# The inverse stage's DFT in one partition half instead of two, and a filter load issued later

## The reference

```python
z = short_conv(u @ w_in + b_in, conv_w, conv_b)
x0, x1, v = jnp.split(z, 3, axis=-1)
s = v * x1
g = hyena_filter(L, ...)                       # (2L, D), L = 1024
y = irfft(rfft(s, n=2L, axis=1) * rfft(g, n=2L, axis=0), n=2L, axis=1)[:, :L]
y = (y + s * skip) * x0
return y @ w_out + b_out
```

## Time and profile before

| | us |
|---|---|
| median of 3 runs | 2532.4 |
| lowest, highest | 2531.71, 2537.66 |
| the profiled execution, its own time | 2537.66 |
| its span in the trace | 2535.2 |
| TensorE busy | 2429.3 (96%) |
| VectorE, GpSimd, ScalarE busy | 1124.9, 705.3, 634.2 |
| `sfwd` ends, `spec` runs | about 336, then to 526.7 |
| `inv` runs (TensorE) | 537.6 to 564.9 |

### The profile page before, as it was taken

How to read it: one execution, slowest core, us unless ns; L and a number is a source line. 1 busy time by engine, 2 the same in 40 slices (tenths; PEclk the granted TensorE clock), 3 DMA queues, 4 the chain that set the end, 5 groups by cost and what they waited for, 6 DMA issues and landing times.

```text
span 2535.2 us, 28807 instructions
## 1 busy us (share of the span) xinstructions
PE 2429.3 (96%) x11294; PEld 1959.1 (77%) x11294; DVE 1124.9 (44%) x1181; ACT 634.2 (25%) x768; POOL 705.3 (28%) x394
## 2 busy tenths in 40 slices
PE   7999999979999999999998899999999999999996
PEld 5767766547888888888887698989897887778885
DVE  6755543254266116622347763627272123420533
ACT  4433423342211000100113544444453001111111
POOL 2221233322233333333334122121212332333331
PEclk9999999999999999999999899999999999999998
DMA  4122354681222122211112202011113322111331
GB/s 148 34 100 100 117 190 158 196 236 42 75 92 90 50 75 99 83 50 66 47 47 73 92 26 74 26 67 33 67 33 119 138 79 67 54 42 66 99 117 66
DMA packets 69969, 217.62 MB, mean 86 GB/s; under 512 B 6662, under 2 KB 16584, under 8 KB 69642
## 3 DMA queue, kind: packets, MB, share of 16 engines
q1 hardware_dynamic: 57002, 178.88, 21.4%
q10 hardware_dynamic: 12896, 37.75, 4.0%
HBM read 171.52 MB, written 45.09 MB: 85 GB/s over the span
## 4 chain that ended last, share of the span: by engine, by line
PE 72%; DVE 4%; ACT 1%; issue 0%; ACTq 0%; DVEq 0%
PE ps L1208 61%; PE ps L541 5%; DVE T L1888 1%; PE ps L1479 1%; PE ps L588 1%; PE ps L609 1%; PE ps L608 1%; PE ps L570 1%; PE ps L607 1%; PE ps L1230 0%; DVE X L2227 0%; DVE XN L1918 0%; PE ps L1239 0%; PE ps L512 0%; ACT T L1771 0%; DVE H L1911 0%
## 5 line engine op out<-in xcount | busy, mean ns | idle before, releaser
L1208 PE MATMUL ps<-H,whi 128*128 128x512 f32 x4000 | 1086.6, 394 | 21.9 <-DVE H L1955 13.1
L1208 PEld LDWEIGHTS ps<-H,whi 128*128 128x128 f32 x4000 | 751.2, 189 | 195.1 <-issue 25.1
L1162 POOL CAST whi<-wraw 128x1024 fp32r<-128x1024 f32 x190 | 201.3, 1059 | 1703.6 <-PE ps L1208 805.9
L1208 PE MATMUL ps<-H,wlo 128*128 128x512 f32 x2000 | 617.9, 390 | 0.0
L1164 POOL TENSOR_TENSOR wlo<-wraw,whi 128x1024 fp32r<-128x1024 f32 x194 | 492.1, 2536 | 58.4 <-ACT whi L675 43.1
L1208 PEld LDWEIGHTS ps<-H,wlo 128*128 128x128 f32 x2000 | 376.6, 188 | 78.9
L1208 PE MATMUL ps<-A,whi 128*128 128x512 f32 x1472 | 397.7, 393 | 8.9 <-DVE A L2259 4.9
L1208 PEld LDWEIGHTS ps<-A,whi 128*128 128x128 f32 x1472 | 278.1, 189 | 68.4 <-issue 5.3
L1208 PE MATMUL ps<-A,wlo 128*128 128x512 f32 x736 | 228.3, 392 | 0.0
L1208 PEld LDWEIGHTS ps<-A,wlo 128*128 128x128 f32 x736 | 139.2, 189 | 29.1
L2143 DVE TENSOR_TENSOR T<-ps,T 128x1024 f32<-128x1024 f32 x22 | 26.9, 1224 | 155.8 <-PE ps L1208 155.8
(11 more groups left out here) (337 smaller groups left out, 2500.8 us busy)
## 6 DMA issues: line engine op xcount, KB each, us to landing
wraw<-in_panels SPq DMA_DIRECT2D x181, 512.0 KB, 3.5
mw<-in_modp SPq DMA_DIRECT2D x24, 512.0 KB, 3.5
g<-gsp SPq DMA_DIRECT2D x16, 512.0 KB, 3.2
wraw<-g SPq DMA_DIRECT2D x16, 512.0 KB, 5.9
bs<-s SPq DMA_DIRECT2D x16, 512.0 KB, 4.9
y<-yi ACTq DMA_DIRECT2D x32, 256.0 KB, 5.2
kf<-in_kfft SPq DMA_DIRECT2D x16, 320.0 KB, 3.1
X<-in_xT SPq DMA_DIRECT2D x4, 1024.0 KB, 11.0
```

Of the source, the lines that this page charges most:

```text
L1162: nc.gpsimd.tensor_copy(whi[:, s, :, :], wraw[:, s, :, :]).then_inc(hi_made, 1)
L1208: last = mm(p[:, c * step:(c + 1) * step], w[:, ws, k, :], operand(act, a, k, c * step, step), start=(q == 0 and w is whi and a == 0), sto ...
```

## The change

The `rows` jobs write PSUM partitions 0 to 63 only: a job now covers 4 slices m of 256 channels instead of 8, so there are 16 jobs instead of 8, with 4 matmuls each instead of 8. The copy back writes partitions 0 to 63 of `YB`, one slice for one slice. A `tile` job becomes 16 transposes of 64 x 128 pieces instead of 8 of 128 x 128, with a 64 x 64 identity. The order becomes: rows x4 | rows rows tile rows rows tile, three times | tile tile. VectorE's work is unchanged.

In SP's queue `filter_rows(1)` moves from between `matrices(1)` and the stores of slices 14 and 15 to after `matrices(3)`, just ahead of `x0_weights(1)`.

```diff
--- before.py
+++ after.py
@@ -68,11 +68,12 @@
 
 
 
-INV = [("rows", 0, 256, 8 * _m) for _m in range(2)]
+INV = [("rows", 0, 256, 4 * _m) for _m in range(4)]
 for _c in range(1, 4):
-    for _m in range(2):
-        INV.append(("rows", 256 * _c, 256, 8 * _m))
-        INV.append(("tile", 2 * _c - 2 + _m))
+    for _m in range(4):
+        INV.append(("rows", 256 * _c, 256, 4 * _m))
+        if _m % 2:
+            INV.append(("tile", 2 * _c - 2 + _m // 2))
 INV += [("tile", 6), ("tile", 7)]
 
 
@@ -1011,7 +1012,6 @@
                     sp.wait_ge(aux_done, A0["sfwd"] + sfwd_aux("turn", PAIRS - 1))
                     for g in range(2):
                         matrices(g)
-                    filter_rows(1)
             for m in range(N2 - 4, N2):
                 sp.wait_ge(*sa_out(m))
 
@@ -1032,8 +1032,7 @@
                 signal_in(g)
                 matrices(g + 2)
                 if g:
-                    if g > 1:
-                        filter_rows(g)
+                    filter_rows(g)
                     if g in X0_AFTER:
                         skipped = g + 1
                         x0_weights(g)
@@ -1418,14 +1417,13 @@
                         k = c0 // 256
                         pe.wait_ge(x_in[k], 64)
                     for u in range(T // w):
-                        for h in range(2):
-                            last = mm(p[HALF * h:HALF * h + HALF, u * w:(u + 1) * w], cc("idft"),
-                                      YB[:, m0 + 2 * u + h, c0:c0 + w], start=True, stop=True)
+                        last = mm(p[0:HALF, u * w:(u + 1) * w], cc("idft"), YB[:, m0 + u, c0:c0 + w], start=True, stop=True)
                 else:
                     e, q = j[0], inv_rows(j[0])
                     pe.wait_ge(evac[slot("inv", q)], turn("inv", q) + 1)
-                    for m in range(PAIRS):
-                        last = nc.tensor.transpose(p[:, m * P:(m + 1) * P], YB[:, m, e * P:(e + 1) * P], ident)
+                    for m in range(N2):
+                        last = nc.tensor.transpose(p[:, m * HALF:(m + 1) * HALF], YB[0:HALF, m, e * P:(e + 1) * P],
+                                                   ident[0:HALF, 0:HALF])
                 last.then_inc(aux_done, 1)
             panel_jobs("wout", 2, A, ready=(y_lo, 0))
             project("first", 0, (n2.lo, 0))
@@ -1698,7 +1696,7 @@
 
                     c0, w, m0 = j
                     act.wait_ge(aux_done, A0["inv"] + o + 1)
-                    A_(YB[:, m0 // 2:m0 // 2 + T // w, c0:c0 + w], ps[slot("inv", o)][:, :].rearrange("p (a b) -> p a b", b=w),
+                    A_(YB[0:HALF, m0:m0 + T // w, c0:c0 + w], ps[slot("inv", o)][0:HALF, :].rearrange("p (a b) -> p a b", b=w),
                        ACT.Copy).then_inc(evac[slot("inv", o)], 1)
 
                     if o and INV[o - 1][0] == "tile":
```

## The result

The changed kernel is slower: 2550.24 us median of 4 runs (2546.87 to 2550.8) against 2533.43 of 4 (2531.71 to 2537.66), a ratio of 1.0061, 95% interval 1.0049 to 1.0075, which is 12 to 19 us. Timed again later with the experiments it came to 1.0058 (1.0044 to 1.0071). The forecast was 2553.9 in a range of 2544 to 2560.

What follows compares the result with a forecast made beforehand. TensorE, busy 96% of the span, was taken as the bound. Inverse stage 12.7, late load 7.2 and half clock 1.6 summed to 21.5 us, giving a 2553.9 us median; own range 2549 to 2557, stated range 2544 to 2560.

Steps and rivals of the forecast that it cites:

- What bounds the stage: Inverse stage: TensorE's cycle grows from 2.90 to 5.45 us, above VectorE's 3.77 a tile, so TensorE becomes the bound.
- The lost pairing: Inverse-stage rows jobs: without the other half beside them, records cost 0.213 us each instead of 0.105 (upper bound 0.25).
- The transposes: Inverse-stage tiles: 16 narrow transposes at 0.107 us each, 1.71 us a tile against 0.86; lower bound 0.053 each.
- The case of cheap transposes: Rival, inverse stage: narrow transposes cost half, so the stage's 12.7 us becomes 7.4; total 2548.6 us; chance 0.13.
- ScalarE stays hidden: Inverse stage: 8 extra evacuations of 1.02 us give ScalarE 4.2 us of a 5.45 us cycle, so they stay hidden.
- The seam: End of the inverse stage, where the first panel's part k = 6 waits: moves 12.7 us later (+1/-1.5).
- The load: Second filter-spectra group: moved filter_rows(1) lands at 346.3, split at 349.8, so TensorE starts 7.2 us later (5.5 to 8.4).
- The clock after the stall: Second filter-spectra group: TensorE restarts at half clock for 3.3 us, costing 1.6 us (bounds 0 and 1.7).
- The load was not hidden: Rival at the second filter-spectra group: load arrives before 342.6, TensorE isn't held; sum 12.7, 2545.1 us; chance 0.06.
- The pairing was real: Rival, inverse-stage rows jobs: pairing did nothing, one half runs at 0.107; sum 11.8, 2544.2 us; chance 0.06.
- The clock did not stay low: Rival, inverse stage: clock stays low with half the array unused, 39 us more; 2593 us; chance 0.07.
- absorbed: Rival, after the convolution: later TensorE waits, 14.1 us at L1230, swallow the delay; not slower, 2532.4 us; chance 0.03.

Runs made afterwards that it cites:

- s10: Changed kernel plus 11 matmuls on constants in TensorE's idle time ahead of the inverse stage; ratio 1.0047 (1.0033 to 1.0061) against the kernel before.
- s3: Kernel before, with each rows job's four matmuls of partition half 0 first, then half 1's four, instead of alternating; ratio 1.0008 (0.9999 to 1.0017).
- s4: Kernel before, paired rows jobs kept, but each half copied separately into partitions 0 to 63 and 16 narrow transposes a tile; ratio 0.9990 (0.9978 to 1.0001).
- s11: Changed kernel with the load left early and copies into both partition halves, so 8 wide transposes a tile; ratio 1.0031 (1.0018 to 1.0045) against the kernel before.
- s5: Changed kernel with the load left early and plain matmuls by the 64 x 64 identity replacing transposes; ratio 1.0132 (1.0113 to 1.0150) against the kernel before.
- s1: Kernel before with only filter_rows(1) moved later in SP's queue, inverse stage untouched; ratio 1.0025 (1.0013 to 1.0037).
- s8: Kernel before plus 11 matmuls on constants in TensorE's idle 10.9 us ahead of the inverse stage; ratio 1.0021 (1.0012 to 1.0029).

## Why the prediction was right

The forecast of the time was right, and so were its two main mechanisms. One term, the transposes, was wrong in its reasoning, and the signs below show it.

**What bounds the stage.** Right. VectorE's 3.77 us a tile was the bound before, TensorE's cycle after. The first six `rows` jobs took 12.03 us to the first transposes, forecast 12.0 (its term for the half clock at the start, 1.4, is the 1.5 that s10 takes away).

**The lost pairing** (0.213 a record, bounds 0.105 and 0.25). Right: 3.67 us for 16 records is 0.219 apart, s3 shows the cause with one edit to the order alone, and s4 and s11 divide the rest of the new form from it.

**The transposes.** This is the term that was mis-sized. I took 0.107 a record from L1328, with a lower bound of 0.053; it is 0.067. L1328 is a plain matmul, and s5 shows that the form makes the difference: the same operands cost 0.113 as a plain matmul. The failed step is "with one column to stream, the weight load sets this rate, and the new transposes load 128 columns each": what limits the plain matmul didn't limit the transpose, and the 0.107 of the wide transposes that seemed to agree was no proof of the same limit. Per tile it makes 1.06 us instead of 1.71, a cycle of 4.74 instead of 5.45, and the sixth tile 37.45 - 28.84 = 8.6 us later in the stage instead of 12.6. The case of cheap transposes, which put this at 7.4, was rated 0.13; the truth lies between the two and nearer to it.

**ScalarE stays hidden.** Right for the cycle and wrong at its end. The forecast counted its load (4.2 us, of a cycle that came out at 4.74) and not its order: the copy of the last `rows` job stands behind a rounding copy and a skip term, and the seventh tile waits 1.22 us for it.

**The seam.** Forecast 12.7 us, measured 8.0 between the two profiled executions (53.3 - 45.3) and 9.0 between the averages of B. At the place that the forecast used, the part k = 6 of the first panel, it is (594.13 - 543.92) - (577.74 - 537.63) = 10.1 us: 8.6 for the sixth tile, and 1.5 because TensorE's own queue was late there by more than VectorE. Then the kernel before lost 2 us behind that place. Both come mostly from a term that the sum didn't have: a stretch of half clock in the first panel, of 0 to 6.8 us in the kernels here.

**The load.** Issue, landing and split were forecast at 340.3 less 1.3, 346.3 and 349.8; they came at 338.3, 346.1 and 349.5, and the second group started 11.5 us behind the first instead of 4.9: 6.6 us, forecast 7.2. Ahead of it, L1400's wait for the signal (1.1 us) is gone into the longer wait.

**The clock after the stall** (1.6 us, bounds 0 and 1.7). It fell to 0.50, as forecast. From the restart to the x0 panel's start it is 358.56 - 349.61 = 8.95 us against 351.11 - 342.63 = 8.48. The six spectra records took 1.0 us longer, and half a microsecond of that went into a wait for the x0 panel's split (0.5 us) that the kernel before had there. So 0.5, inside the bounds and a third of the forecast. A as a whole: 7.2 us on average (6.0 between the two profiled executions) where 8.8 were forecast.

**The sum.** 9.0 + 7.2 = 16.2 us against a forecast of 21.5 and 15 to 17 measured, 2550.2 against 2553.9. The side, the lost pairing and the late load were right and each in its place; the sizes of the two halves were 3.7 and 1.6 us too large. That the median lies in the range is in part luck of its width, which took in the forecast and three rivals. The rival of cheap transposes gave 2548.6, nearer to 2550.2 than the forecast's 2553.9. Its sum of 16.2 us is the measured one only by chance: 7.4 for the stage is too little and 8.8 for the load too much.

**The signs that it named.** Two came as written: L1422's records 0.216 us apart, and TensorE's wait ahead of the second group of filter spectra with the clock at 0.50 after it. Two didn't, both from the transposes: a tile's 16 come to 1.06 us and not over 1.7, and the sixth tile moved by 8.6 us and not by 13. The fifth, an unchanged delay from 600 us on, holds up to the heads and not in stretch C, which gave 3.3 us back. The prediction also said that it would be wrong if narrow loads were cheaper. In the transposes the narrow ones were; that part of it is refuted.

**The rivals.** The load was not hidden. The pairing was real. The clock did not stay low. Nothing that was lost was absorbed by a wait for something untouched: from the first panel to the heads every kernel here takes 847 to 848 us.

## What to carry to other kernels

Matmuls that use half of the output partitions are worth twice as much when neighbours in the queue go to different halves; before a layout is simplified to one half, look at the starts of the records and not at their durations, which are the same. When a load is moved in a hand-written queue, count the bytes that now stand ahead of it, those issued right behind it, which share the DMA engines with it, and the engine that takes its jobs in order behind it; the nearest row is the load that had this place before (landed by 347.58, forecast 346.3, measured 346.06). And a limit that is read off a plain matmul need not hold for a transpose, even where the two show nearly the same rate at one shape (0.106 and 0.107 here): leave the range open down to what the other rows allow.

## What the runs showed of the hardware

**The clock decides some microseconds at the seams.** C has no edit in it and takes 28.7, 30.3 to 30.4 or 32.0 us. The windows of the kernel before and of s1 over its first 8 us:

```profile
1431.00:1439.00 8.00, 7.89 (x22) 4.78 (x23) 8.00 (x6) 4.53 (x4) 3.31 (x2) 0.57 0.22 68
```

```profile
1436.00:1444.00 8.00, 8.00 (x37) 5.80 (x38) 8.00 (x6) 5.81 (x6) 3.22 (x1) 1.00 0.21 68
```

At 0.57 TensorE does 22 records of the stretch in 8 us, at 1.00 it does 37. Where the half clock falls changes from one execution to the next, at the seam of the inverse stage too, and a kernel that comes later to such a place can be better off there. It also explains most of why the two profiled spans are only 10.0 us apart after a seam 14.3 us apart: C gave 3.3 of it back. This is likely most of the spread of 15 us between single executions. Each timed execution has its mean granted clock on record, and it goes with the time: of the 35 executions of the kernel before beside s1 to s4, the eight at 0.982 average 2539.7 us, the eight at 0.984 2536.3 and the three at 0.987 2529.1, and the order is the same on the other two chips. Where the half clock fell in them isn't on record. It may also be why the sum of the two halves timed alone (12.1 us) differs from the whole (15); an interplay of the two isn't needed for it, and isn't ruled out by these intervals.

**A transpose of 64 partitions costs more than half of one of 128.** 16 narrow ones start 0.067 us apart; 16 wide ones in a row take 1.97 us, (1.97 - 0.27)/15 = 0.11 apart. The narrow ones have half the partitions and half the moving columns and cost 0.6 of the time; which of the two makes them cheaper, no run here shows.

**The overlap across halves is short.** In s3, with eight records of one half queued ahead of eight of the other, only four of the one ran beside four of the other; in the kernel before, where the halves alternate by matmul, all 16 ran in pairs.

**VectorE beside GpSimd.** In s4 and s8 single L2116 operations (L2119, L2118 there) that usually take 1.23 us took 2.95 to 3.21 us while GpSimd split panels. That is in the stage's middle and cost nothing where TensorE was the bound.
